# Rows of reciprocal roots for the out-projection through DRAM instead of products with diagonals

## The reference

```
h    = rmsnorm(x) ; proj = h @ w_in
attn = rmsnorm(dilated_attention(q, k, v)) * silu(z_attn)         # 16 heads x 128
y    = ssd forward + ssd backward + d_skip * xs ; y = y * silu(z_ssm)
ssm  = rmsnorm(y in 4 groups of 512) * ssm_norm_g
mix  = concatenate([attn, ssm]) @ w_out                           # 4096 -> 2048
out  = x + rmsnorm(mix)
```

## Time and profile before

| | |
|---|---|
| runs of before | 2436.77, 2437.54, 2440.17 us (median 2437.54) |
| profiled execution | 2437.86 us, span 2436.1 us |
| PE, DVE, ACT, POOL busy | 99%, 71%, 40%, 16% of the span |
| chain that ended last | PE 85%; DVE, DMA, ACT 1% each |
| DMA | 379.43 MB, 156 GB/s on average |

### The profile page before, as it was taken

How to read it: one execution, slowest core, us unless ns; L and a number is a source line. 1 busy time by engine, 2 the same in 40 slices (tenths; PEclk the granted TensorE clock), 3 DMA queues, 4 the chain that set the end, 5 groups by cost and what they waited for, 6 DMA issues and landing times.

```text
span 2436.1 us, 37150 instructions
## 1 busy us (share of the span) xinstructions
PE 2405.7 (99%) x13708; PEld 2284.2 (94%) x13708; DVE 1731.5 (71%) x2435; ACT 979.3 (40%) x1622; POOL 389.5 (16%) x580
## 2 busy tenths in 40 slices
PE   7999999999999999999999999999999999999998
PEld 6999999999999999999999999999999988888887
DVE  5686765555565555564787888788878768787767
ACT  6323433333333333333445444544454533234332
POOL 0000444444444444440000000000000000000000
PEclk9999999999999999999999999999999999999999
DMA  4235455555555555555464546554654435443544
GB/s 162 79 108 162 152 163 155 163 155 158 163 155 166 155 155 155 155 157 199 151 190 143 179 142 188 172 152 142 192 167 133 145 112 180 156 156 121 170 165 159
DMA packets 316776, 379.43 MB, mean 156 GB/s; under 512 B 20006, under 2 KB 237286, under 8 KB 313751
## 3 DMA queue, kind: packets, MB, share of 16 engines
q1 hardware_dynamic: 265063, 222.06, 29.9%
q10 hardware_dynamic: 33200, 106.02, 13.1%
q0 software_dynamic: 18432, 50.36, 6.6%
HBM read 299.16 MB, written 86.54 MB: 158 GB/s over the span
## 4 chain that ended last, share of the span: by engine, by line
PE 85%; DVE 1%; DMA 1%; ACT 1%; issue 0%; ACTq 0%; DVEq 0%; SPq 0%
PE ps L1012 35%; PE ps L810 22%; PE ps L1165 14%; PE ps L1085 4%; PE ps L971 2%; PE ps L938 2%; PE ps L905 2%; PE ps L921 1%; PE ps L981 1%; DMA w_raw<-in_w_in 1%; PE ps L945 0%; PE ps L912 0%; PE ps L954 0%; PE ps L994 0%; PE ps L1207 0%
## 5 line engine op out<-in xcount | busy, mean ns | idle before, releaser
L1012 PE MATMUL ps<-h_hi,w_hi 128*128 128x384 f32 x960 | 322.5, 336 | 0.0
L1012 PE MATMUL ps<-h_lo,w_hi 128*128 128x384 f32 x960 | 322.0, 335 | 0.0
L1012 PE MATMUL ps<-h_hi,w_lo 128*128 128x384 f32 x960 | 321.7, 335 | 0.0
L2194 DVE TENSOR_TENSOR w_lo<-raw_qk,w_hi 128x512 fp32r<-128x512 f32 x240 | 183.3, 764 | 182.7 <-ACT w_hi L1538 181.7
L810 PE MATMUL ps<-h_hi,w_hi 128*128 128x384 f32 x1056 | 275.1, 341 | 0.0
L1245 ACT ACTIVATE w_hi<-w_raw 128x512 fp32r<-128x512 f32 x176 | 109.9, 628 | 400.3 <-PE ps L810 271.2
L810 PE MATMUL ps<-h_lo,w_hi 128*128 128x384 f32 x1056 | 268.9, 335 | 0.0
L810 PE MATMUL ps<-h_hi,w_lo 128*128 128x384 f32 x1056 | 268.8, 335 | 0.0
L1012 PE MATMUL ps<-t_hi,w_hi 128*128 128x384 f32 x720 | 243.4, 338 | 0.9 <-DVE w_lo L2194 0.7
L1012 PE MATMUL ps<-t_hi,w_lo 128*128 128x384 f32 x720 | 243.5, 338 | 0.0
L1012 PE MATMUL ps<-t_lo,w_hi 128*128 128x384 f32 x720 | 242.6, 337 | 0.0
(11 more groups left out here) (327 smaller groups left out, 5183.9 us busy)
## 6 DMA issues: line engine op xcount, KB each, us to landing
raw_qk<-in_w_in SPq DMA_DIRECT2D x90, 512.0 KB, 4.3
w_raw<-in_w_in SPq DMA_DIRECT2D x176, 256.0 KB, 3.6
stage<-loc_scr ACTq DMA_DIRECT2D x16, 1536.0 KB, 7.3
stage<-t_scr SPq DMA_DIRECT2D x48, 512.0 KB, 3.6
stage<-in_w_out POOLq DMA_DIRECT2D x144, 128.0 KB, 2.8
t_scr<-stage POOLq DMA_DIRECT2D x144, 128.0 KB, 2.3
stage<-in_w_out SPq DMA_DIRECT2D x36, 512.0 KB, 3.7
stage<-zx_scr ACTq DMA_DIRECT2D x46, 384.0 KB, 8.9
```

The costliest lines, as they stand in the source:

```text
L1012: ins = nc.tensor.matmul(ps[:, bank, 0:HALF_T], w, h(k), start=(start and kk == 0 and q == 0), stop=(last and kk == KC - 1 and q == 2), sk ...
L2194: nc.vector.tensor_tensor(w_lo[:, n_slot(n, pp), :], src, w_hi[:, n_slot(n, pp), :].bitcast(f32), ALU.subtract).then_inc(w_lo_done, 1)
```

## The change

Each root goes to DRAM and comes back as a row. ACT stores the 128x6 tile into a row of a new scratch tensor `r_scr` (4 x 768), token by token, on its own DMA queue, and later loads that row into all 128 partitions: the attention row into `osq_sum`, the others one after the other into `w_raw` columns T to 2T, where the diagonals were. The diagonals, the four pairs of products, ACT's copy of the attention row and their semaphores are gone. `mean_and_root` waits for the store of the last root before it writes its place again. In phase 3 of step 1 DVE sums one square in each of units 2, 3, 4 and 5.

```
-            diag_done, ... pe.wait_ge(att_row, 1) ... pe.wait_ge(um_done, GRP)      # in sums_of_squares
-            def roots_to_rows(n, halves):
-                pe.wait_ge(diag_done, n + 1)
-                for th, half in enumerate(halves):
-                    last = nc.tensor.matmul(ps[:, 6 + th, 0:HALF_T], ones, half, start=True, stop=True)
-                last.then_inc(row_ready, 1)
-            def diagonals(j, n, halves):
+            def store_root(j, n):
                 act.wait_ge(r_ready, j + 1)
-                for t in range(TT):
-                    at = t % (TT // 2) * P
-                    last = nc.scalar.activation(halves[t // (TT // 2)][:, at:at + P], ident, ACT.Copy,
-                                                scale=r_of(j)[:, t:t + 1])
-                last.then_inc(diag_done, 1)
+                act.dma_start(r_scr[n].rearrange("(t p) -> p t", p=P), r_of(j), allow_slow_non_contiguous=True).then_inc(r_stored, 16)
+            def load_root(n, row):
+                act.wait_ge(r_stored, 16 * n + 16)
+                if n > 1:
+                    act.wait_ge(um_done, (GRP, 2 * GRP)[n - 2])
+                act.dma_start(row, r_scr[n:n + 1, :].rearrange("a t -> (a t)").partition_broadcast(P)).then_inc(r_row_in, 16)
...
             root(STAT_ATT)
+            store_root(STAT_ATT, 0)
             squares_of(0, 1, 1)
-            diagonals(STAT_ATT, 0, (diag_att[:, 0:HALF_T], diag_att[:, HALF_T:T]))
+            load_root(0, r_att_row)
             w2_split(2)
-            act.wait_ge(row_ready, 1)
-            nc.scalar.activation(r_att_row..., ps[:, 6:8, 0:HALF_T], ACT.Copy).then_inc(att_row, 1)
...
                 if step == BLOCK_STEPS - 1 and j == 5 * PHASE_B:
-                    sp.wait_ge(row_ready, 4)
+                    sp.wait_ge(um_done, 2 * GRP * BLOCK_STEPS)
...
                 if j > STAT_SECOND:
-                    dve.wait_ge(diag_done, j - 1)
+                    dve.wait_ge(r_stored, 16 * (j - 1))
...
+                    if step == 1 and p == 3 and i >= 2:
+                        add_square(1, 3, 2, i - 2)
                     if i in (2, 3):
                         for k in (2 * (i - 2), 2 * (i - 2) + 1):
-                            if step == 1 and p == 3:
-                                add_square(1, 3, 2, k)
```

More of the change, by code:

```diff
@@ L169, in encoder @@
             alog_f, alog_b, d_skip, ssm_g, w_out, post_g, squares, hots,
-            zx_scr, y12_scr, t_scr, u_scr, brow_scr, strip_scr, loc_scr, er_scr, cb_scr, y_prompt, y_sample):
+            zx_scr, y12_scr, t_scr, u_scr, brow_scr, strip_scr, loc_scr, er_scr, cb_scr, r_scr, y_prompt, y_sample):
     f32, f32r = mybir.dt.float32, mybir.dt.float32r
@@ L333, in encoder @@
         usq = w2_second[:, 0:T]
-        diag_att = w2_second[:, T:2 * T]
-        diag_ssm = (w2_second[:, 2 * T:2 * T + HALF_T], stage[:, TT * D_MODEL + 2 * WG + MG:TT * D_MODEL + 2 * WG + MG + HALF_T])
-        r_att_row = osq_sum[:, :]
+        r_att_row, r_ssm_row = osq_sum[:, :], w2_second[:, T:2 * T]
         usq_first = (strip[:, 0:T], zs)
@@ L401, in encoder @@
         sum_in, sum_done, sum_out = sem("sum_in"), sem("sum_done"), [sem(f"sum_out{i}") for i in range(3)]
-        diag_done, row_ready, att_row, um_done = sem("diag_done"), sem("row_ready"), sem("att_row"), sem("um_done")
+        r_stored, r_row_in, um_done = sem("r_stored"), sem("r_row_in"), sem("um_done")
         g_in = sem("g_in")
@@ L1098, in sums_of_squares @@
                     pe.wait_ge(stat_read, j)
[L1099 to L1102, removed]
                 src = osq_sum if j == STAT_ATT else ssum
@@ L1177, in block_steps @@
                                 sums_of_squares(STAT_LAST)
-                            if step == 1 and p == 6 and i == 1:
-                                pe.wait_ge(unit_added, UNIT_ADDED + STEP_UNITS + 6 * PHASE_UNITS)
-                                roots_to_rows(3, diag_ssm)
             def last_step():
@@ L1725, in _ @@
             root(STAT_ATT)
+            store_root(STAT_ATT, 0)
             squares_of(0, 1, 1)
-            diagonals(STAT_ATT, 0, (diag_att[:, 0:HALF_T], diag_att[:, HALF_T:T]))
+            load_root(0, r_att_row)
             w2_split(2)
-            act.wait_ge(row_ready, 1)
-            nc.scalar.activation(r_att_row.rearrange("p (h t) -> p h t", h=2), ps[:, 6:8, 0:HALF_T], ACT.Copy
-                                 ).then_inc(att_row, 1)
             root(STAT_SECOND)
-            diagonals(STAT_SECOND, 1, diag_ssm)
+            store_root(STAT_SECOND, 1)
             squares_of(1, 2, 1)
+            load_root(1, r_ssm_row)
             w2_split(3)
@@ L1739, in _ @@
             root(STAT_THIRD)
-            diagonals(STAT_THIRD, 2, diag_ssm)
+            store_root(STAT_THIRD, 2)
             for b in range(2, PHASE_B):
                 b_round(b)
+            load_root(2, r_ssm_row)
             for f in range(BLOCK_STEPS * PHASES):
@@ L1749, in _ @@
                         a_round(f + 1, h)
+                    if step == 1 and p == 5:
+                        load_root(3, r_ssm_row)
                     if step == 1 and p == 3:
@@ L1755, in _ @@
                     root(STAT_LAST)
-                    diagonals(STAT_LAST, 3, diag_ssm)
+                    store_root(STAT_LAST, 3)
                 if step == BLOCK_STEPS - 1 and p in (4, 5):
@@ L2386, in normalise @@
                 kt = group * GRP + k
-                u = u_buf[n][:, k * T:(k + 1) * T].rearrange("p (h t) -> p h t", h=2)
+                u = u_buf[n][:, k * T:(k + 1) * T]
                 if row is None:
                     dve.wait_ge(u_buf_in[n], X_IN + 16 * times)
-                    dve.wait_ge(att_row, 1)
-                    by = r_att_row.rearrange("p (h t) -> p h t", h=2)
-                else:
-                    dve.wait_ge(row_ready, row + 1)
-                    by = ps[:, 6:8, 0:HALF_T]
+                    dve.wait_ge(r_row_in, 16)
+                    by = r_att_row
+                else:
+                    dve.wait_ge(r_row_in, 16 * row + 16)
+                    by = r_ssm_row
                 nc.vector.scalar_tensor_tensor(u, u, mix_cols[:, kt:kt + 1], by, ALU.mult, ALU.mult).then_inc(um_done, 1)
```

12 lines of the change are left out of this document (1 added, 11 removed).

## The result

The new kernel is slower by 0.15%, not faster by 0.31%: its median is 2442.84 us (17 runs, 2439.61 to 2446.86) against 2438.3 us for before (17 runs beside it), ratio 1.0015 with an interval of 1.0008 to 1.0021 (the two medians alone give 1.0019). Forecast (2430.0) and range (up to 2434.0) are both missed. By the bound of 0.2% that the prediction named this is no change, which had a chance of 0.12; by the interval it is a small but real loss, and 13 us above what was forecast.

What follows compares the result with a forecast made beforehand. TensorE was taken to bound the kernel, busy 2405.7 of 2436.1 us. Savings of 6.40 + 0.15 + 1.06 = 7.6 us gave a forecast of 2430.0 us, 0.31% less, range 2428.0 to 2434.0.

Steps and rivals of the forecast that it cites:

- The pairs and the first wait: Four pairs of full-precision ones-times-diagonal products on PE, and its wait for the first diagonals, go: 6.40 us saved.
- the PSUM row: PE's third sum of squares no longer waits for DVE to read the row in PSUM: 0.15 us saved.
- rival D: Out-projection and later: the removed products could have been hidden beside other products; judged excluded, with no chance given.
- The squares: Phase 3 of step 1: one square per unit on DVE removes a PE wait with its restart, 1.06 us saved.
- The store: Each root's 768 separate 4-byte values go to DRAM on ACT's queue: taken as 4.7 us, bounded by 2.1 and 10.
- Row 1 falls within the same shift: Second root's trip, with 11 us for its store: a slow store there adds no delay beyond row 0's.
- Rival C: Slower: from an 11 us store on, ACT's split and PE are late; 2450.6 us at 22 us; chance 0.04.
- The row's load: Load of 3 KB into all 128 partitions: taken as 4 us, bounded by 2.6 and 8.9.
- ACT's freed time: ACT loses 24 diagonal copies and one row copy; it gains time but bounds nothing.
- the readers from SBUF: DVE's multiplications by the rows cost the same from SBUF as from PSUM: 3.78 us for four.
- the gain's load: Post-norm gain's load waits for step 1's last multiplication of a u by its root; free in SP's order.
- The signs: Listed trace observations that would show the forecast right or wrong, such as PE idle before a column block for ACT's split.

Runs made afterwards that it cites:

- turned sums: The changed kernel with SSD sums made as six rows of 128, stored as 512-byte runs, and the attention load behind the split: 2432.09 us, ratio 0.9967.

## Why the prediction was wrong

- **The pairs and the first wait, 6.40 us, and the PSUM row, 0.15.** Right. Of the 7.75 us in the kernel with 24-byte runs, 0.78 to 0.9 are the squares; 6.8 to 7.0 are left for these terms, against 6.55. That the pairs could be hidden (rival D) is out.
- **The squares, 1.06 us.** Right but for 0.3: 0.78 alone. DVE's one idle of 1.86 us stands where it was foreseen.
- **The store, "I take 4.7".** This is the step that failed. It took 11.6, 9.6, 9.6 and 11.4 us in after, and up to 14.4 with the loads behind. Its bounds of 2.1 to 10 came from packets of other queues times a count, and the count turned out not to matter (8.8 us for 128 neighbours, 2.2 for 768 values far apart). The rule that I weighed, from the Trainium skill, "DMA: Bandwidth & Descriptors", section "Specifications" (a read-modify-write below 512 bytes), pointed the right way but does not separate the cases: the 24-byte and the spread 4-byte stores are far below 512 bytes too and land in 1.4 to 4.2 us for rows 1 to 3 (5.6 and 6.8 for row 0), and no store took the 17 us that doubling gave.
- **"Row 1 falls within the same shift", and 11 us for it, counted with DVE on time.** The limits for PE were sound, the chain was missing. ACT hands its lateness to DVE, DVE makes the next root late, and that root's store starts late. Put together with the measured lateness of each root and less what PE has lost by then, the prediction's own limits give waits of 11.6 - 11 = 0.6 us for row 0 (1.0 measured), 3.25 + 9.6 - 11 - 1.0 = 0.85 for row 1 (1.15), and 7.1 + 16.7 - 16.4 - 3.85 = 3.55 for row 2 (3.65). With the loads behind the splits PE has no wait for rows 0 and 1, which shows that the order on ACT hands it on; there row 1 still makes DVE late by its own reader (2.51 us), a path that the prediction doesn't have, and through it row 2.
- **Rival C had the mechanism and not its price.** By its terms a store of 9.6 to 11.6 us costs 0.6 us at most (11.6 - 11, at row 0). The waits and what followed them cost 10.45 us, of which 4.45 are slower products behind the second and third wait, a term that stood nowhere in the prediction: a wait of 3.65 us was a loss of 6.4.
- **The row's load, "I take 4".** 3.7 to 5.7 us for rows 0, 1 and 3, but 7.0 for row 2, where it counts: by the limit above that is 3.0 of the 3.65 us that PE waits there. Behind a quick store the same load, issued earlier, takes 3.8 us (24-byte runs) and 3.3 (turned sums).
- **ACT's freed time, the readers from SBUF, the gain's load.** Right: ACT is busy 7.5 us less (979.3 to 971.8) and nothing comes of it; four multiplications take 3.81 us, 3.78 before; no wait for the post-norm's gain appeared.
- **The signs.** "PE idle before a column block for ACT's split" and "DVE waiting for w_raw from DRAM for more than 7 us" both came (0.87 and 1.01 us; 9.92 us) and named the cause at once. I had given that rival, C, 0.04.

Open stay why single values side by side are slow to store, and some 0.8 us of the 11.2 that the account of waits doesn't hold.

## What to carry to other kernels

A transfer that the trace doesn't show should be bounded by its form in DRAM, and here the count of packets said nothing: turn the data so that a run is at least 8 bytes, better a whole row of partitions, before the kernel stands in a queue for it. A wait for a transfer in an in-order queue holds all that is behind it, so put the consumer's load behind the work that PE needs, and count the slack of the second and third trip from when they really start. And a wait of TensorE is priced with what follows it: here 1.7 and 2.75 us of slower products behind waits of 1.15 and 3.65, and nothing behind the single ones of 0.87, 1.10 and 1.61.

## What the runs showed of the hardware

- Stores of 4-byte values next to each other landed in 8.5 to 14.4 us, whether 128, 384 or 768 of them. 8 bytes or more apart, or as runs of 8 bytes or more, 768 values took 1.4 to 4.2 us for rows 1 and 2, and 3.3 to 6.8 for rows 0 and 3, with the same number of packets where they were apart.
- The load of a row of 3 KB into 128 partitions took 3.2 to 7.5 us, and once 11.4 (row 0 with the loads behind the splits).
- PE's granted clock stayed at 1.00 after single idle times of 0.74 and 0.79 us, 0.75 in the kernel with fewer values, 0.87 in after, and 1.10 and 1.61. It fell to the 1.2 GHz level behind 1.01 us that stood right behind 1.39 us of one-column products and 18 us after the 0.87 (which of the two matters isn't shown), and behind 3.14, 3.48, 3.65 and 4.79 us. Products were back at 0.227 us each 3.1 to 6.0 us after the first one behind the wait.
- A reciprocal on DVE takes 4.95 us for 128x768 (6.4 ns a column), 0.94 for 6x128, 0.19 for 128x6.
- The unchanged program before the out-projection ended anywhere from 1951.2 to 1955.9 us, a spread as large as the effects looked for; counted from a landmark to the end, two kernels whose program ahead of it differed by 1.9 us both show 477.0.
